# Context modulation products on TensorE, the context branch from expert block 0 on, and gated totals in the last block of a three-layer MoE and mixer kernel

## The reference, cut to what matters

```python
# first block
mod = silu(c) @ w_ada + b_ada
h = rms_norm(x, norm1_g) * (1 + scale1) + shift1
proj = h @ w_in                     # 8 heads of kind A, 4 of kind B (two score maps each)
x = x + gate1 * (concat(o_a, o_b) @ w_out)
h2 = rms_norm(x, norm2_g) * (1 + scale2) + shift2
y = moe_ffn(h2)                     # per expert: clipped gate and up, down; top 4 of 32
x = x + gate2 * y
# second block, layers l = 0 and 1
mod  = silu(c_2)     @ ada_w_2[l] + ada_b_2[l]      # for x
modc = silu(c_ctx_2) @ ada_w_2[l] + ada_b_2[l]      # for the context
hc = modulate(rms_norm_2(xc, mix_pre_g[l]), shc1, scc1)
pc = hc @ w_in_2[l]                 # context: conv gates, qkv, gmlp, branch gates
x  = x  + g1 * rms_norm_2(mixer_merge(p, ...), mix_post_g[l])
xc = xc + gc1 * rms_norm_2(mixer_merge(pc, ...), mix_post_g[l])    # layer 0 only
x  = x  + g2 * rms_norm_2(sq_relu_mlp(h2, w_ff1[l], w_ff2[l]), ffn_post_g[l])
```

## Time and profile before

| | |
|---|---|
| median of 3 runs | 3182.68 us |
| the profiled execution's own time | 3185.1 us |
| its span, first to last instruction | 3183.0 us |
| busy: TensorE, VectorE, ScalarE, GpSimd | 93%, 44%, 15%, 2% of the span |
| bytes moved | 752.86 MB, 237 GB/s in the mean |
| mean granted TensorE clock | 0.969 of full |

### The profile page before, as it was taken

One profiled execution on the slowest core, in us unless ns is written; L12 is line 12 of the kernel. 1 busy time (PEld: TensorE's weight loads), 2 busy tenths in 40 slices (PEclk: granted clock), 3 DMA queues, 4 the chain that ended last, 5 costly groups with the idle time before them and its releaser, 6 DMA issues.

```text
span 3183.0 us, 30698 instructions
## 1 busy us (share of the span) xinstructions
PE 2962.6 (93%) x11852; PEld 1736.1 (55%) x11852; DVE 1385.6 (44%) x3322; ACT 473.9 (15%) x943; POOL 61.2 (2%) x93
## 2 busy tenths in 40 slices
PE   5977789999999999999879999899999899999998
PEld 2464224455555555555457768544444577586764
DVE  5755453245557412111236853262763358641101
ACT  1212000012121211100111131100000111311100
POOL 0000000000000000000000000000000000000000
PEclk9967999999999999999989999999999999999999
DMA  8524999999999898999944313343432244124242
GB/s 332 204 113 171 419 422 401 377 380 376 379 385 389 358 375 340 373 370 371 369 189 159 145 67 128 137 146 112 172 138 93 91 151 155 53 106 159 106 159 92
DMA packets 107151, 752.86 MB, mean 237 GB/s; under 512 B 12352, under 2 KB 12736, under 8 KB 18272
## 3 DMA queue, kind: packets, MB, share of 16 engines
q1 hardware_dynamic: 92592, 682.66, 54.3%
q0 software_dynamic: 8064, 54.53, 4.5%
q10 hardware_dynamic: 6352, 13.71, 1.2%
HBM read 741.68 MB, written 9.18 MB: 236 GB/s over the span
## 4 chain that ended last, share of the span: by engine, by line
PE 80%; DMA 11%; DVE 6%; ACT 2%; issue 1%; POOL 0%; DVEq 0%; SPq 0%; ACTq 0%
PE ps L519 27%; PE ps L531 17%; DMA ring<-stream 10%; PE ps L794 9%; PE ps L709 8%; PE ps L875 6%; PE ps L705 3%; PE ps L549 2%; PE ps L801 1%; PE ps L578 1%; DVE area L1097 1%; DMA area<-modulation 1%; PE ps L1000 1%; PE ps L980 1%; PE ps L809 1%
## 5 line engine op out<-in xcount | busy, mean ns | idle before, releaser
L519 PE MATMUL ps<-area,ring 128*128 128x256 f32 (+1 forms) x3456 | 863.8, 412 | 0.3
L519 PEld LDWEIGHTS ps<-area,ring 128*128 128x128 f32 x3456 | 659.2, 191 | 201.4 <-issue 122.5
L531 PE MATMUL ps<-ring,area 128*128 128x512 f32 x1344 | 581.2, 593 | 1.0 <-DVE area L2011 1.0
L794 PE MATMUL ps<-ring,area 128*64 128x512 f32 x2112 | 480.2, 600 | 42.7 <-DMA ring<-stream 41.6
L531 PEld LDWEIGHTS ps<-ring,area 128*128 128x128 f32 x1344 | 255.5, 191 | 316.8 <-issue 314.0
L794 PEld LDWEIGHTS ps<-ring,area 128*64 128x64 f32 x2112 | 146.7, 138 | 357.3 <-issue 266.5
L709 PE MATMUL ps<-area,ring 128*128 128x256 f32 x1152 | 254.7, 379 | 0.8 <-DMA ring<-stream 0.8
L875 PE MATMUL ps<-ring,area 128*64 128x512 f32 x1056 | 240.8, 609 | 11.9 <-ACT area L2236 10.9
L709 PEld LDWEIGHTS ps<-area,ring 128*128 128x128 f32 x1152 | 216.1, 190 | 28.9 <-issue 1.1
L1786 DVE SCALAR_TENSOR_TENSOR area<-area,cols 128x256 f32<-128x256 f32 x480 | 202.6, 484 | 1.1
L875 PEld LDWEIGHTS ps<-ring,area 128*64 128x64 f32 x1056 | 74.0, 139 | 158.3 <-issue 140.4
(11 more groups left out here) (329 smaller groups left out, 2002.8 us busy)
## 6 DMA issues: line engine op xcount, KB each, us to landing
ring<-stream SPq DMA_DIRECT2D x626, 1024.0 KB, 9.0
area<-shared_modulation POOLq DMA_DIRECT2D x48, 1024.0 KB, 8.8
area<-modulation SPq DMA_DIRECT2D x16, 1536.0 KB, 6.6
expert_rows<-area ACTq DMA_DIRECT2D x62, 128.0 KB, 7.4
x<-x_tiles ACTq DMA_DIRECT2D x1, 1024.0 KB, 12.7
area<-ctx_tiles ACTq DMA_DIRECT2D x1, 1024.0 KB, 4.9
out<-x SPq DMA_DIRECT2D x1, 1024.0 KB, 3.9
cst<-constants ACTq DMA_DIRECT2D x1, 928.5 KB, 13.7
```

What stands on the lines that cost most here:

```text
L519: i = mm(ps[:, b, 0:n], w[:, k % 4, j * P:(j + 1) * P], rhs(k), start=(k == 0), stop=(k == 4 * kgs - 1))
L531: i = mm(ps[:, b, :], lhs(k, t), w[:, k % 4, :], start=(k == 0), stop=(k == 4 * kgs - 1))
L794: i = mm(ps[half(h), bank, :], xT[:, k % 4, half(k // 4)], w[:, 2 * (k % 2) + h, :], start=(k == 0), stop=False)
```

## The change

1. **The first eight shared chunks** (2048 columns: the context's and x's shift and scale) leave the expert blocks. They are streamed through the ring as eight chunks `pair` between `w_in` and `w_out`, and TensorE multiplies them: 4 products of 8 matmuls, 512 columns wide, with the two conditions spread over 2 x 32 columns of a 64 wide stationary (`condb`), even and odd k on the two halves of the array. ScalarE copies each product to SBUF, TensorE adds the halves and turns it with 4 matmuls against a two column selector (`fold_pair`), VectorE copies 8 columns. Products lie before and inside `weigh` of B heads 0 to 3. The B heads keep two score banks, not four.
2. **The remaining 16 chunks** go one per block, blocks 0 to 15. START is 0, so the planner lays the context steps from block 0 on. By its own rules the plan becomes:

| blocks | heavy steps | before |
|---|---|---|
| none | 0, 1, 31, 32 | 0 to 5, 32 |
| one | 10, 13, 14, 18, 21, 23, 26, 28 | 17, 31 |
| two | 2 to 9, 11, 12, 15, 16, 17, 19, 20, 22, 24, 25, 27, 29, 30 | 6 to 16, 18 to 30 |

3. **VectorE's order** before the A heads: squares and norms of group 0 first, then sums 6 and 7, squares and norms of group 1, take 0, sum 8, take 1. Sum 9 moves between the A heads, which get `sums(3)` for one of their `sums(2)`.
4. **The end of the experts**: four gather buffers instead of two; rows 4 to 7 are taken in block 32 ahead of its gate; `yacc` is gated and added to `x` while block 32's down product runs; block 32's output is multiplied by the gate on VectorE (in place of ScalarE's copy) and its scattered rows are added straight to `x`. ScalarE makes two more half copies for that (`gate2h`).

```diff
-START = 4
+START = 0
+FIRST = 8
+PAIRG = 4
 def mods_in(e):
-    return [(e, n) for n in range(2 if e < START else 1)]
-MOD_AT = [at for e in range(NBLK) for at in mods_in(e)][:MODS]
+    return [(e, 0)]
+MOD_AT = [None] * FIRST + [at for e in range(NBLK) for at in mods_in(e)][:MODS - FIRST]
...
     put("w_in", 12)
+    put("pair", 2 * PAIRG)
     put("w_out", 4)
...
-        came = [v(25088 + D * n, D) for n in range(2)]
+        came = [v(at_, D) for at_ in (25088, 26112, 18880, 19904)]
+        gate2h = v(20928, 512)
...
+            def pair_products():
+                for n in range(PAIRG):
+                    b = claim("side", ("pair", n))
+                    pe.wait_ge(*at("condb"))
+                    for k in range(KD):
+                        c = CH["pair"] + 2 * n + k // 4
+                        w = chunk(c)
+                        i = mm(ps[64 * (k % 2):64 * (k % 2) + 64, b, :], condb[:, k, :], w[:, k % 4, :], start=(k < 2), stop=(k >= KD - 2))
+                        closed(i, ("pair", n), c, k % 4 == 3, k == KD - 1)
+                        yield
...
+            def fold_pair(n):
+                b = claim("aux", ("pairs", n))
+                pe.wait_ge(*at(("drained", ("pair", n))))
+                for j in range(4):
+                    i = mm(ps[:, b, 2 * j:2 * j + 2], pairb[n % 2][:, j * P:(j + 1) * P], con("pairsel", 2), start=True, stop=True)
...
-            banks["acc"] = (0, 1, 2, 3)
             for h in range(B_HEADS + 1):
...
+                pair_rows(KD // 2)
                 if h:
-                    weigh(("B", h - 1), 2560 + P * (h - 1), P)
+                    weigh(("B", h - 1), 2560 + P * (h - 1), P, lambda: pair_rows(KD // 2))
                     close_sums(("ada", h), FOLDS[h - 1], claim("aux", ("ada", h)))
+                    fold_pair(h - 1)
+                else:
+                    pair_rows(KD // 2)
+            banks["acc"] = (0, 1, 2, 3)
...
             for m in range(2):
-                for g in ((6, 7), (8, 9))[m]:
-                    whole_sums(g)
                 for t in range(TT):
                     head_squares(m, t)
                 head_norms(m)
-            for m in range(2):
-                take_heads(m)
+                if m:
+                    take_heads(0)
+                for g in ((6, 7), (8,))[m]:
+                    whole_sums(g)
+            take_heads(1)
+            for s in range(2):
+                V.tensor_copy(condb[:, :, 32 * s:32 * s + 32], cond[:, 8 + 8 * s:16 + 8 * s].unsqueeze(2).to_broadcast([P, KD, 32])).then_inc(*mark("vector_steps", *(["condb"] if s else [])))
...
                     take_mod(("ada", h), MODF * FOLDS[h - 1][0], MODF * len(FOLDS[h - 1]))
+                    dve.wait_ge(*at(("full", ("pairs", h - 1))))
+                    V.tensor_copy(mod2w[:, 8 * (h - 1):8 * h], ps[:, B(("pairs", h - 1)), 0:8]).then_inc(*mark("modulation_read", ("drained", ("pairs", h - 1))))
...
+                    for m in range(TOPK, TT * TOPK):
+                        take_rows(m)
                 dve.wait_ge(*at((tag, "gate")))
...
+                if not upcoming:
+                    dve.wait_ge(*last("sums_updated"))
+                    dve.wait_ge(*at(("drained", "gate2b")))
+                    gated_totals()
+                    dve.wait_ge(*last("x_updated"))
+                    dve.wait_ge(*at((tag, "chunk", CPE - 1)))
+                    TT_(ysb, ps[:, 1, :], gate2h, ALU.mult).then_inc(*mark("last_rows_ready", (tag, "y")))
...
+                act.wait_ge(*at(("full", ("pair", h))))
+                if h >= 2:
+                    act.wait_ge(*at(("full", ("pairs", h - 2))))
+                A(pairb[h % 2], ps[:, B(("pair", h)), :], ACT.Identity).then_inc(*mark("products_copied", ("drained", ("pair", h))))
...
             for n in range(TT * TOPK):
-                if n >= 2:
-                    pool.wait_ge(*at(("taken", n - 2)))
+                if n >= 4:
+                    pool.wait_ge(*at(("taken", n - 4)))
```

More of the change, by code:

```diff
@@ L306, in build @@
         rows_stored = K.sem("expert_rows_stored")
-        rows_came = [K.sem(f"expert_rows_came{s}") for s in range(2)]
+        rows_came = [K.sem(f"expert_rows_came{s}") for s in range(4)]
         shared_landed = K.sem("shared_modulation_landed")
@@ L586, in products, with pair_rows @@
                     next(later, None)
+            def pair_rows(n):
+                for _ in range(n):
+                    next(pairs_, None)
+            def fold_pair(n):
[3 more added lines that the diff above has]
+                    i = mm(ps[:, b, 2 * j:2 * j + 2], pairb[n % 2][:, j * P:(j + 1) * P], con("pairsel", 2), start=True, stop=True)
+                i.then_inc(*mark("modulation_full", ("full", ("pairs", n))))
             def head(key, q, k, hp, lo):
@@ L1244, in _ @@
                 else:
-                    sums(2)
+                    sums(3)
             def outB(h):
@@ L1699, in _ @@
                 expert(("moe", e), e, lambda key: at((prev, key)), e > STORED, e >= STORED, e < NE, True, context_at(e))
-            dve.wait_ge(*last("rows_taken"))
             for t in range(TT):
-                summed(("end", "moe"), t)
+                tag = ("end", "moe")
+                dve.wait_ge(*at((tag, "s", t)))
+                for h in range(2):
+                    xs = x[:, t, 512 * h:512 * h + 512]
+                    i = TT_(xs, xs, ps[:, 6 + h, :], ALU.add)
+                i.then_inc(*mark("sums_updated", (tag, "y+", t)))
             for e in range(NBLK, NBLK + 8):
@@ L1709, in _ @@
                 K.prefix = "spill_"
+                V.memset(yacc, 0.0).then_inc(*mark("vector_steps"))
+                dve.wait_ge(*last("vector_steps"))
                 for p in range(1, NPASS):
@@ L1722, in _ @@
                 dve.wait_ge(*last("sums_updated"))
+                gated_totals()
+                dve.wait_ge(*last("x_updated"))
                 K.prefix = ""
             dve.wait_ge(*last("sums_updated"))
-            dve.wait_ge(*at(("drained", "gate2b")))
-            for t in range(TT):
-                TT_(yacc[:, t, :], yacc[:, t, :], gate2b, ALU.mult).then_inc(*mark("vector_steps"))
-                dve.wait_ge(*last("vector_steps"))
-                TT_(x[:, t, :], x[:, t, :], yacc[:, t, :], ALU.add).then_inc(*mark("x_updated", ("x2", t)))
+            V.tensor_copy(stat("done"), flag[:, 0:1]).then_inc(*mark("x_updated", *[("x2", t) for t in range(TT)]))
             for t in range(TT):
@@ L2238, in expert @@
                 work("l2")
+                if not upcoming:
+                    return
                 act.wait_ge(*at((tag, "chunk", CPE - 1)))
@@ L2419, in _ @@
             pool.wait_ge(*at(("part", MOD1 - 1)))
-            for m in range(MODS):
-                if m:
+            for m in range(FIRST, MODS):
+                if m > FIRST:
                     pool.wait_ge(*at(("part2", m - 1)))
@@ L2580 @@
     put("w_in", a["w_in"][0])
+    put("pair", a["ada_w_2"][0][:, 0:512 * PAIRG])
     put("w_out", a["w_out"][0])
```

40 lines of the change are left out of this document (24 added, 16 removed).

## The result

The changed kernel runs in **3149.73 us**, the median of 4 runs (3145.45 to 3153.71). The kernel before took 3183.35 us beside it, the median of 4 (3181.11 to 3188.72). The ratio is **0.9892 [0.9873, 0.9911]**: faster by 33.6 us, or 1.1%. The forecast was 3139, in a range of 3117 to 3162. The profiled execution took 3145.45 us (span 3143.6) against 3185.1, so 39.65 us are to be found between the two traces. The profiled execution lies 4.3 us under the median of its runs after, and 1.8 us over it before, which is the difference between 39.65 and 33.6.

A forecast was written before the change was run, and what follows sets the result against it. It took early expert blocks as bound by bytes, later ones by TensorE. Terms -39.3, -8.2, +8 and -4.4 sum to -43.9 us, from 3185.1 to 3141.2; with the runs' median 2.4 lower it predicted 3139 us, range 3117 to 3162.

The forecast's parts named there:

- Part 3: B heads: the added pair products and their folding cost 8 us, between +2 at full clock and +10 at half clock.
- block 31: Experts' stage: no heavy step, 12 chunks, taken at 30 us, with up to 40 if the gathers come close by.
- Part 1: Experts' stage: earlier context steps and 8 chunks fewer bring the intervals from 1286.6 to 1247.2 us, a gain of 39.3.
- One-heavy blocks: Blocks 18, 21, 23, 26, 28, one heavy step and 13 chunks: 34 us each, 170 in all.
- The blocks with two heavy and few light ones: Blocks 22, 24, 25, 27, 29, 30: 40.3 us each, 242.0 in all, priced by blocks 24 to 30 before.
- Part 2: Ahead of the A heads: VectorE's norms first bring the first scores 8.8 us earlier, net gain 8.2 us.
- a clock of 1.00: B heads: sign that the forecast is wrong, TensorE's clock at 1.00 there, a gain of 6 to 8 us more.
- Part 4: End of the experts: TensorE resumes 4.4 us earlier, with bounds of 1 and 6.5 us.
- Bytes set the stage: Rival, experts' stage: the ring reaches 385 GB/s, so eight chunks fewer give 22 us, total 3156 us; chance 0.18.
- The waits go too: Rival: most of the 41.6 us of ring waits end as well, 24 us more gain, total 3115 us; chance 0.12.
- The ring's refill binds: Rival, mainly B heads: exposed chunk loads lose 60 us, total 3199 us, slower; chance 0.04.
- the rule of the Trainium skill: Experts' stage: HBM transfers bind near 358 GB/s, so 8 chunks fewer would give 23 us whatever is laid where.

The follow-up runs named there:

- e3: Changed kernel without the eight gathers of expert rows, VectorE's sums taking data already in SBUF: 3140.04 us, ratio 0.9855.
- e8: Changed kernel with expert 30 also scattered through TensorE, so gathers start in block 30, and the planner's quota putting single heavy steps in place B: 3136.05 us, ratio 0.9845.
- e9: Changed kernel with only the planner's quota changed, so that a block's single heavy step falls to place B: 3142.52 us, ratio 0.9869.
- e4: Changed kernel with VectorE's old order ahead of the A heads, sums ahead of norms: 3162.15 us, ratio 0.9922.
- e5: Changed kernel with the old end: totals gated after the last scatter, ScalarE copying block 32's output, no half copies: 3152.97 us, ratio 0.9907.
- e1: Changed kernel with START at 4 again, context steps from block 4 on, shared chunks staying where the change puts them: 3164.86 us, ratio 0.9927.
- e2: Changed kernel with each of the 16 shared chunks loaded twice into the same buffer: 3173.14 us, ratio 0.9955.
- e7: Changed kernel with experts 0 to 29 stored and expert 30 scattered through TensorE, so the gathers can start in block 30: 3144.87 us, ratio 0.9878.
- e10: The changed kernel itself, unchanged, timed again in a later series: 3150.17 us, ratio 0.9891.
- e11: Changed kernel with gathers starting in block 30 and the quota putting single heavy steps in place B, timed again: 3135.93 us, ratio 0.9843.

## Why the prediction was right

It was right in direction and range, and in the mechanism of parts 1, 2 and 4; the point was 10.7 us too low. Part 3 came out near by luck: its work was priced at about half, and a clock that it did not expect made up for it. Two more gains, 3.4 and 1.7 us, which lie mostly or wholly in the clock, offset a part of what block 31 lost. Step by step:

- **Part 1, the experts' stage: mechanism right, 12.2 us too much.** The classes of blocks, forecast and measured: 0 and 1, 64.1 and 65.0; two heavy and a shared chunk, 461.4 and 459.2; one heavy and a shared chunk, 109.6 and 111.7; 16, 17, 19, 20, 170.1 and 170.6; 22 to 30 with two heavy, 242.0 and 236.7; 18, 21, 23, 26, 28 with one, 170 and 176.2; block 31, 30 and 40.07. Six of seven are within 6.2 us, and these six cancel to 2.2. **The step that failed is block 31**: "I take 30, since six chunks lie ready after a block of two heavy steps." The bound of 40 beside it was right. The chunks ahead shorten the wait at the start of a block; they don't take away the 4.2 MB of gathers that land in it. e3 showed this by removing them.
- **One-heavy blocks** were to take 34. Four of the five took 33.3 to 34.8, and block 23 took 39.4 (37.7 to 40.6 in the other traces with this plan). That one is no matter of bytes: with place B empty nothing covered VectorE's part of a light step. An empty place B alone does no harm: 18 and 28 have it too, without light steps, and took 33.3 and 34.1. The sum counted heavy steps per block, and neither where they lie nor which light ones stand beside them; with the quota of e8 and e9 block 23 took 35.2.
- **The blocks with two heavy and few light ones** took 39.5, not 40.3. The price was a mean over blocks 24 to 30 of before, and block 25 there (41.15) held the two light steps `bc` that now stand in block 23. So some of this gain is the loss of block 23. Blocks 29 and 30 had 41.5 and 40.8; why was not tested.
- **Part 2, VectorE's order: right.** Forecast 8.8 at the first scores, measured 8.5, and taken back by e4 alone (8.3). In the ten other traces with this order the first scores stand at 93.5 to 95.2.
- **Part 3, the pair products: near in size, by luck.** Forecast last turns 208.3, measured 206.7. From the first scores to there 6.7 us more, forecast 8.6. The forecast took "32 take 7.09 us" from a row that counts records and applied it to 32 written matmuls, which are 64 records; the folding was priced the same way. So it had (3.5 + 0.85) us per head at half clock, 17.4 in all. From the B heads' first scores (171.57 us before, 163.26 after) to the last turns the rows of the changed kernel show 24.6 us for both, though half of the products' records or more ran at the upper level. Against that, 8.2 us of TensorE's idle time were covered, and the old rows of this stretch took 18.2 us instead of 28.1: the granted clock rose to 0.73 (0.53 in the earlier trace rows), which the forecast had not taken. 24.6 - 8.2 - 9.9 is 6.5. What it named as what would make it wrong (a clock of 1.00, 6 to 8 us) came in part.
- **Missed: 302 us came 3.4 us early.** Nothing of the change lies between the B heads and block 0's reading, and the forecast priced it at nothing. Some 3 us of it are 32 matmuls of one line, which take 6.88 us before and 3.83 after. It is no accident of one trace after the change: in all twelve traces of changed code this stretch takes 96.1 to 97.3 us, against 99.5 in the only one of before. The granted clock there: 0.50 before and 0.69 after from 250 to 260 us, 0.73 and 0.88 from 282 to 303. The matmuls and the windows of the changed kernel and, below, of the kernel before:

```profile
252.46 3.83 PE L688 MATMUL ps<-area 128*128 128x32 f32 x32
...
250.00:260.00 10.00, 9.70 (x61) 9.29 (x59) 6.61 (x25) 1.62 (x7) 0.00 (x0) 0.69 0.14 44
282.00:303.00 21.00, 20.08 (x86) 6.85 (x87) 11.60 (x35) 3.29 (x5) 0.54 (x1) 0.88 0.68 268
```

```profile
253.17 6.88 PE L652 MATMUL ps<-area 128*128 128x32 f32 x32
...
250.00:260.00 10.00, 10.00 (x49) 10.00 (x48) 3.71 (x8) 0.00 (x0) 0.00 (x0) 0.50 0.14 60
282.00:303.00 21.00, 19.38 (x70) 5.98 (x69) 12.95 (x39) 6.78 (x12) 0.54 (x1) 0.73 0.48 174
```

- **Part 4, the end: 6.9 us, forecast 4.4**, just beyond the bound of 6.5. The moved passes gave 2.2 (e5). The down product and a scatter at the higher clock level gave 2.6 (e5's list), which the forecast left out, and the 1.7 of the down product are luck: in the eleven traces with this end it took 7.09 to 9.58 us and the end 25.8 to 28.8, so the gain is 3.9 to 6.9, and 5.2 with a down product as long as before. e5 and the changed kernel had the same 7.09, so their difference of 2.2 holds.
- **The rivals.** *Bytes set the stage* would have given 22 us in the experts and both kernels of e1 alike; the early plan gave 17.9 by itself. But bytes do set single blocks: 0 to 8 at the margin (e2), and 31 outright (e3). *The waits go too*: they went from 41.6 to 30.7 us, a quarter of it. Its own sum was wrong: its three terms (5 x 1.5, 3 x 2.5 and 6) are 21 us and not 24, so 3118. *The ring's refill binds*: no row of the pair products waits for the ring, and a chunk lands in 8.7 us. As to the rule of the Trainium skill that was cited, the changed kernel shows 420 GB/s in block 31 once more. The Trainium skill's page "HBM Reference", section "Specifications (TRN2)", says that 358 GB/s is a core's share while both cores of a pair stream, and that one alone gets about 425: the trace of this one-core kernel agrees.

The sum was 44, and 33.6 were measured (39.65 between the two profiled executions). The 6 us between those two are where the profiled executions lie in the spread of their runs.

## What to carry over

Price a block by what is due in it on every resource: by the bytes of all queues together, gathers and stores included, by its TensorE work, and by where in the block that work lies. Chunks that lie ready carry a stage over a wait, not over bytes that exceed the block's time. When a price is read from a trace, count the new work in the trace's records too and not in the program's instructions. When steps are laid out by a quota, look at the blocks that get one: another quota was worth 3.0 to 8.5 us, about as much as moving the gathers out of block 31 (4 to 5). And where equal code differs by 3 to 5 us, compare the stages that differ, not the totals.

## What the runs showed of the hardware

- **Equal code differs by 5 us, and the granted clock with it.** In ten traces that are equal up to there the last turns of the B heads came at 201.94 and 202.17 us (e9, e8) or between 205.30 and 207.13 us (the changed kernel, e1, e2, e3, e5, e7, e10, e11). From the first scores it was 108.4 us in the two and 111.6 to 111.9 in the eight. The granted clock of 163 to 213 us was 0.80 and 0.81 in the two and 0.74 in the eight; the same eight records of a pair product took 1.94 us in e9 and 3.68 in the changed kernel. The window of e9:

```profile
163.00:213.00 50.00, 48.18 (x258) 31.77 (x256) 36.34 (x101) 12.84 (x42) 0.00 (x0) 0.81 0.67 269
```

- **A busy TensorE was granted the lower clock level.** From 255 to 260 us the kernel before was busy 5.00 of 5 us at 0.50, and of 250 to 260 us 10.00 of 10 at 0.50, with 49 matmul records. The changed kernel, busy for 9.70 us of the same 10, had 0.69. From 213 to 250 us, ahead of that, the two run the same work at 0.95 to 0.97 and at 0.90 to 0.93, so these runs don't show what makes the difference.
- **TensorE can wait for the ring while the DMA engines have room.** In 368 to 660 us it waited 11.7 or 23.1 us at the same 382 GB/s and the same share of 0.94 (e2).
